# Half-width products, copies and subtractions in the chunk-matrix inverse of a hybrid decoder layer

## What is computed

```python
    m = a_mat + jnp.eye(c, dtype=F32)
    u = lax.linalg.triangular_solve(m, v * beta[..., None], left_side=True, lower=True, unit_diagonal=True)
    w = lax.linalg.triangular_solve(m, kb * jnp.exp(gam)[..., None], left_side=True, lower=True, unit_diagonal=True)
```

## Time and profile before

| | us |
|---|---|
| runs | 5926.58, 5926.8, 5918.99; median 5926.58 |
| the profiled execution: its own time | 5921.17 |
| its span in the profile | 5919.5 |
| PE busy (matmul) | 5294.7 (89%) |
| DVE, ACT, POOL busy | 2368.5, 1498.2, 784.4 |
| mean granted TensorE clock | 0.917 of full |

### The profile page before, as it was taken

The page is one execution under the profiler, slowest core; times in us unless marked ns, Lnnn a source line. Parts: engine busy times, 40 slices in busy tenths (PEclk is TensorE's granted clock), DMA queues, the critical chain, the costliest instruction groups (busy, mean ns, idle before and its releaser), DMA issues. The chain is left out here.

```text
span 5919.5 us, 91242 instructions
## 1 busy us (share of the span) xinstructions
PE 5294.7 (89%) x34908; PEld 3261.9 (55%) x34908; DVE 2368.5 (40%) x5479; ACT 1498.2 (25%) x3418; POOL 784.4 (13%) x1063
## 2 busy tenths in 40 slices
PE   8988999995777756889999899998999999989998
PEld 5644445554555542565555655565555655657554
DVE  1156655543445436253433534335333443321322
ACT  2235443432223210121212212122122221211212
POOL 0012221111443310110001101011010110100000
PEclk9989999997987855889999899998999989998998
DMA  3111011104776620312223122232233122241332
GB/s 97 48 31 36 29 33 35 35 32 137 227 223 193 181 70 9 105 43 72 86 72 102 51 73 84 77 84 62 73 87 93 54 76 74 75 130 51 95 94 69
DMA packets 729154, 487.80 MB, mean 82 GB/s; under 512 B 78058, under 2 KB 704106, under 8 KB 728687
## 3 DMA queue, kind: packets, MB, share of 16 engines
q1 hardware_dynamic: 677457, 393.53, 23.3%
q0 software_dynamic: 18432, 50.36, 2.9%
q10 hardware_dynamic: 32832, 38.09, 1.9%
HBM read 432.76 MB, written 49.09 MB: 81 GB/s over the span
## 5 line engine op out<-in xcount | busy, mean ns | idle before, releaser
L3368 PE MATMUL s_f_b<-s_f_h,s_f_W 128*128 128x416 f32 x4480 | 1640.8, 522 | 31.1 <-DMA s_f_h<-o_t 22.1
L3368 PEld LDWEIGHTS s_f_b<-s_f_h,s_f_W 128*128 128x128 f32 x4480 | 845.8, 192 | 708.7 <-issue 691.3
L3426 PE MATMUL s_f_b<-s_f_a,s_f_W 128*128 128x416 f32 x1760 | 634.1, 516 | 0.2
L536 PE MATMUL s_p_acc<-s_hT,s_p_W 128*128 128x416 f32 x1600 | 626.3, 539 | 6.9 <-DMA s_p_W<-in_w_in_dram 6.9
L3426 PEld LDWEIGHTS s_f_b<-s_f_a,s_f_W 128*128 128x128 f32 x1760 | 328.5, 190 | 263.5 <-issue 257.4
L536 PEld LDWEIGHTS s_p_acc<-s_hT,s_p_W 128*128 128x128 f32 x1600 | 300.1, 196 | 286.2 <-issue 269.5
L3624 DVE TENSOR_TENSOR s_f_xT<-s_f_xT,s_f_b 128x416 f32<-128x416 f32 x160 | 93.5, 586 | 587.1 <-PE s_f_b L3426 533.3
L3645 POOL TENSOR_TENSOR s_f_ex<-s_f_ex,s_f_mix 128x416 f32<-128x416 f32 x105 | 111.8, 1065 | 1348.9 <-ACT s_f_mix L3454 1348.3
L918 ACT ACTIVATE s_prob<-s_s_ps,s_ntop 128x512 f32<-128x512 f32 (+3 forms) x320 | 196.4, 619 | 368.2 <-DVE s_ntop L969 368.0
L3497 ACT ACTIVATE s_f_raw<-s_f_b 128x416 f32<-128x416 f32 x110 | 56.9, 517 | 774.9 <-PE s_f_b L3368 774.9
L1165 POOL DMA_DIRECT2D s_V<-in_cache_diff_v_dram x384 | 207.6, 541 | 278.5 <-issue 274.9
(11 more groups left out here) (790 smaller groups left out, 8010.0 us busy)
## 6 DMA issues: line engine op xcount, KB each, us to landing
s_f_W<-in_ffn_w_in_dram SPq DMA_DIRECT2D x220, 512.0 KB, 3.9
s_K<-in_cache_diff_k_dram SPq DMA_DIRECT2D x512, 128.0 KB, 2.9
s_V<-in_cache_diff_v_dram POOLq DMA_DIRECT2D x384, 128.0 KB, 3.2
s_f_W<-in_ffn_w_out_dram SPq DMA_DIRECT2D x80, 448.0 KB, 3.8
cols_t<-s_p_out ACTq DMA_DIRECT2D x100, 208.0 KB, 1.9
s_f_W<-in_w_out_dram SPq DMA_DIRECT2D x40, 512.0 KB, 4.6
s_f_W<-in_ffn_w_out_dram SPq DMA_DIRECT2D x40, 512.0 KB, 4.1
s_V<-in_cache_diff_v_dram ACTq DMA_DIRECT2D x128, 128.0 KB, 3.3
```

Of the source, the lines that this page charges most:

```text
L536: mm = pe.matmul(self.acc[n % 2][:, 0:CH], self.W[:, u, k, :], self.hT[:, k, c * CH:(c + 1) * CH], start=(k == 0), stop=(k == KD - 1))
L3368: mm = pe.matmul(bank(u)[:, 0:G], w[:, k, :], h[:, k, :], start=(k == 0), stop=(k == KD - 1 and kind != "op"))
L3426: mm = pe.matmul(bank(u)[:, 0:G], w[:, k, :], a[:, f % NA, :], start=(k == 0), stop=(k == len(part) - 1))
```

## The change

The left operand of a level is nonzero only in a triangular block pattern, so a level changes only half of the columns of X (the even blocks of 2^b columns) and of XT (the odd blocks). After the change the moving operand of each product is only that half: `left` streams 32 columns of X into a packed half bank, `right` streams 32 columns of Y and 32 of XT. The stationary operands stay 64x64. ScalarE copies 192 columns instead of 384 and spreads them into Y; VectorE subtracts 192 columns instead of 384. As Y is also a stationary operand, its other columns have to be zero: each level has a Y of its own (5 x 6 x 64 = 1920 columns), set to zero once by GpSimd. In the paged stage that buffer lies over the memory K/V tile that is written later; in the last stage it is allocated. The number of matmuls, copies and subtractions is the same.

```diff
+    def side(self, x, r, h, b, right):
+        return x[r, h, :].rearrange("p (k a s) -> p k a s", a=2, s=2 ** b)[:, :, right, :]
+    def sides(self, x, b, right):
+        return x.rearrange("p h (k a s) -> p (h k) a s", a=2, s=2 ** b)[:, :, right, :]
+    def cell(self, bank, r, h, b):
+        return bank[r, h * HD // 2:(h + 1) * HD // 2].rearrange("p (k s) -> p k s", s=2 ** b)
+    def cells(self, bank, b):
+        return bank[:, 0:W_A // 2].rearrange("p (k s) -> p k s", s=2 ** b)
...
     def left(self, pe, bank, b):
         for h, r in self.each():
-            mm = pe.matmul(self.view(bank)[r, h, :], self.AM[b % 2][r, h, :], self.X[r, h, :], start=True, stop=True)
+            mm = pe.matmul(self.cell(bank, r, h, b), self.AM[b % 2][r, h, :], self.side(self.X, r, h, b, 0),
+                           start=True, stop=True)
         return mm
     def right(self, pe, bank_x, bank_xt, b):
         for h, r in self.each():
             if b < self.LEVELS:
-                pe.matmul(self.view(bank_x)[r, h, :], self.XT[r, h, :], self.Y[r, h, :], start=True, stop=True)
-            mm = pe.matmul(self.view(bank_xt)[r, h, :], self.Y[r, h, :], self.XT[r, h, :], start=True, stop=True)
+                pe.matmul(self.cell(bank_x, r, h, b), self.XT[r, h, :], self.side(self.Y[:, b - 1, :, :], r, h, b, 0),
+                          start=True, stop=True)
+            mm = pe.matmul(self.cell(bank_xt, r, h, b), self.Y[r, b - 1, h, :], self.side(self.XT, r, h, b, 1),
+                           start=True, stop=True)
         return mm
+    def keep_y(self, act, bank, b):
+        return act.activation(self.sides(self.Y[:, b - 1, :, :], b, 0), self.cells(bank, b), ACT.Copy)
+    def less_x(self, dve, bank, b):
+        x = self.sides(self.X, b, 0)
+        return dve.tensor_tensor(x, x, self.cells(bank, b), ALU.subtract)
+    def less_xt(self, dve, bank, b):
+        x = self.sides(self.XT, b, 1)
+        return dve.tensor_tensor(x, x, self.cells(bank, b), ALU.subtract)
...
# in rwkv_lanes and in gdn_lanes
+    Y = C.y_home(st, "r_Y")
+    blank = st.sem("r_blank")
...
             if slot[0] == "Y":
+                if t == 0 and slot == "Y1":
+                    act.wait_ge(blank, 1)
                 need(act, T, slot, t)
-                go(inv.Y[:, :, :], inv.view(B[0]), ACT.Copy)
+                inv.keep_y(act, B[0], int(slot[1:])).then_inc(A.sem, 1)
...
                 if b < inv.LEVELS:
-                    dve.tensor_tensor(inv.X[:, :, :], inv.X[:, :, :], inv.view(B[1]), ALU.subtract)
-                tt(inv.XT[:, :, :], inv.XT[:, :, :], inv.view(B[2]), ALU.subtract)
+                    inv.less_x(dve, B[1], b)
+                inv.less_xt(dve, B[2], b).then_inc(V.sem, 1)
...
     def pool_lane(pool):
+        pool.memset(Y[:, :, :, :], 0.0).then_inc(blank, 1)
...
# homes of Y: in the stage of the paged attention, and in the last large stage
+                C.y_home = lambda st, name: mem_kv[:, 0:5 * 6 * HD].rearrange("p (b h d) -> p b h d", b=5, h=6)
+                    C.y_home = lambda st, name: st.sb(name, [P, 5, 6, HD])
```

More of the change, by code:

```diff
@@ L2435, in rwkv_lanes @@
     oT = st.sb("r_oT", [P, 3, P])
-    inv = Scan64(C.levels, C.eye, six(rs), six(Dx), six(kp), (six(G_), six(ep)))
+    Y = C.y_home(st, "r_Y")
+    blank = st.sem("r_blank")
+    inv = Scan64(C.levels, C.eye, six(rs), six(Dx), Y, (six(G_), six(ep)))
     B = [st.ps(f"r_b{j}", [P, 512]) for j in range(3)]
@@ L2850, in gdn_lanes @@
     six = lambda x: x.rearrange("p c (a d) -> p (c a) d", d=HD)
-    inv = Scan64(C.levels, C.eye, six(rs[:, 0:3, :]), E[:, :, :], six(rs[:, 3:6, :]), (gB[:, :, :], Eb[:, :, :]))
+    Y = C.y_home(st, "g_Y")
+    blank = st.sem("g_blank")
+    inv = Scan64(C.levels, C.eye, six(rs[:, 0:3, :]), E[:, :, :], Y, (gB[:, :, :], Eb[:, :, :]))
     B = [st.ps(f"g_b{j}", [P, 512]) for j in range(3)]
@@ L3998, in build @@
                 C.g_mem, C.g_ffn, C.g_final = g_mem, g_ffn, sb("g_final", [P, KD])
-                C.mK_T, C.mV = sb("mK_T", [P, MH, MEM]), sb("mV", [P, 2, MI])
+                mem_kv = sb("mem_kv", [P, MH * MEM + 2 * MI])
+                C.mK_T = mem_kv[:, 0:MH * MEM].rearrange("p (h m) -> p h m", m=MEM)
+                C.mV = mem_kv[:, MH * MEM:].rearrange("p (c n) -> p c n", n=MI)
+                C.y_home = lambda st, name: mem_kv[:, 0:5 * 6 * HD].rearrange("p (b h d) -> p b h d", b=5, h=6)
                 ss = Stage(nc).__enter__()
```

## The result

The changed kernel takes 5955.66 us (median of 4 runs, 5948.5 to 5958.1) against 5926.59 on the same chip: ratio 1.005, 95% interval 1.0033 to 1.0068. It is slower, by about 29 us; the forecast was no change. The profiled execution took 5955.97 us, 34.8 more than that of before (5921.17).

What follows compares the result with a forecast made beforehand. PE, busy 89% of the span, bounds the kernel. From 5921.2 us, edges -8-3, evictions -5-2, clock +12+6 and GpSimd +1 gave 5922; weighed with the runs shown, 5924 us, range 5888 to 5956.

Steps and rivals of the forecast that it cites:

- the clock term: TensorE's clock falls as less is streamed: +12 us in the last stage's memory attention, +6 in the paged stage.
- The third rival: Clock drops last through four blocks' memory attention and the paged stage's inverse groups: 5946 us; chance 22%.
- Pace: In the 10752 inverse matmuls, weights set the pace, so starts stay 0.030 us apart: 0 saved.
- The first rival: Pace follows the moving columns, so 10752 records save 0.015 us each: 5775 us; chance 5%.
- Edges: Inverse groups start and end faster, 0.05 us for both edges: -8 us in the last stage, -3 in the paged.
- Copies and subtractions: Shorter evictions cut PE's waits: -5 us in the paged stage, -2 in the last.
- The third rival's detail: Once at the lower level, a 32-column stretch does not bring the clock back up.
- GpSimd: Four memsets of some 1.7 us; the one ahead of V-page loads in the paged stage costs +1 us.

Runs made afterwards that it cites:

- e1: Changed kernel with all products streaming 64 columns again, copies and subtractions still 192 scattered columns; 5923.14 us, ratio 1.0004 to the kernel before.
- e5: Changed kernel with 64-column products in the paged stage and the last stage's four memory-attention tiles, 32 in its other eight; 5918.16 us, ratio 0.9995.
- e4: Changed kernel with 64-column products only in the last stage's four memory-attention tiles, 32 everywhere else; 5942.05 us, ratio 1.0032 to the kernel before.
- e3: Changed kernel with only the left products at 32 columns, the right ones at 64, evictions 192; 5929.52 us, ratio 1.0011 to the kernel before.

## Why the prediction was wrong

The forecast was 5924 us, no change; it came out 5955.66, at the upper edge of the range. The step that failed is the clock term, +18 us, where the profiles show about 45: 32 in the memory attention and 13 in the paged stage. The third rival, "the clock takes more" (5946 us, 22%), is what happened, with its own sign met, a last stage at 0.95 or below: it is at 0.95.

- **Pace, 0 saved: right.** 24 records of 32 columns last 0.89 us, 0.92 before. The first rival is out.
- **Edges, -11: too large.** Two neighbouring groups save 0.03 us together, not 0.05 at each exit (to the next feed matmul it is 0.14 us, for 0.15 before and 0.13 forecast), and the dense stretches between the attentions show 1.6 us less in all.
- **Copies and subtractions, -7: right in size where it was looked for.** The paged waits fell by 7 us, 8 if each lost its full share; the paged stage gains about 6 (mean of seven profiles). Missed was that e1 gives the same amount back in the memory attention, where its clock is lower.
- **The clock, +18: the step that failed.** The text took a stretch of 24 us at 0.99 and let it fall to the 0.83 of its neighbour: +12 over four blocks. In fact the neighbour fell too, to 0.71, and the four blocks lost 31.9 us. Set against kernels with the same evictions and 64 columns (637.3 to 643.4 us for four blocks), some 19 to 25 of that come from the narrow products; the other 7 to 13 are there with short evictions alone. In the paged stage, +6 was forecast from a guessed 0.80 and a third of the effect; the profiles show +13 and the medians (e5 to e4) +24. The direction was right and the size was not: the neighbour's 0.83 was no level that a stretch can rest at; it was a mean over pieces at 0.5 and pieces at 1.0, and the same change moved it.
- **The third rival's detail: partly wrong.** It said that once down, a narrow stretch doesn't bring the clock back. It comes back, for 6 us at a time, and falls again at 3308.
- **GpSimd, +1:** the new memsets take 1.7 us each as forecast, and no wait of PE on them stands in the trace.

By stage against 5921.2: paged stage +5, sample rows -1, attention +32, dense stretches -2, rest +1, so 5956; the profiled execution took 5955.97.

**What stays open:** why half-width evictions alone cost 3 us of clock in each of blocks 2 to 4 (e1), why e3, with a third of the products narrow, has the shorter memory attention, and why unread products bring 26 us on e1 and about 4 on the kernel before. That 32-column products in the paged stage and in the memory attention cost clock is shown by the runs; by what rule the clock falls is not. All three questions seem to be about where in a stretch the falls come, which no run here varied by itself.

## What to carry to other kernels

Before halving what a matmul streams, ask whether streaming sets its pace. Where the weights do (here the starts of neighbouring 64x64 matmuls stood equally far apart at 6, 32 and 64 columns), fewer columns save nothing on PE and can cost clock; then the other half may as well be streamed and thrown away. Look for this where the granted clock already goes up and down: among matmuls of 416 columns it cost nothing that can be told, in stretches at 0.8 to 0.9 it cost 20 us or more twice. And when a clock term is estimated from a neighbouring stretch, ask whether that stretch would move too.

## What was not expected of the hardware

- The clock can fall or hold behind the same 1.36 us of idle time in the same order of matmuls: 0.51 over the next 10 us in the changed kernel, groups at full pace (0.92 and 0.87 us) in e1. The width of the products before it isn't the only difference, as PE comes there at another moment; but in none of the 16 blocks with 64 columns and short evictions did the clock fall in the first 51 us, and in all 12 with 32 columns it did within 40.
- Matmuls of 64x64 in the idle half of the array's rows are free in time: 24 records in the 0.91 us of 12. With half-width evictions and 372 of them the time is 0.37% below that of the kernel before (0.9963, 0.9952 to 0.9973), with 732 it is 0.55% below (0.9945, 0.9928 to 0.9961), although nobody reads what they compute.
